# Scores of the sample attention: keys turned in place by VectorE and multiplied on sixteen array tiles

## The reference, cut to what matters

```python
kp = cache_k[page_table].reshape(DB, past, H, Dh)
vp = cache_v[page_table].reshape(DB, past, H, Dh)
suffix = (lax.cumsum(lfp, axis=1, reverse=True) - lfp).transpose(0, 2, 1)
s_past = jnp.einsum('bqhd,bkhd->bhqk', q, kp) * scale
s_past = s_past + suffix[:, :, None, :] + cn[:, :, :, None]
s_new = jnp.einsum('bqhd,bkhd->bhqk', q, k) * scale
s_new = s_new + cn[:, :, :, None] - cn[:, :, None, :]      # causal
p = softmax(concat([s_past, s_new]))
o = einsum(p[..., :past], vp) + einsum(p[..., past:], v)
```

## Time and profile before

| what | us |
|---|---|
| median of 3 runs | 1962.62 |
| lowest, highest | 1959.45, 1966.36 |
| span of the profiled execution (the page has no other time of it) | 1963.6 |
| first instruction of the stage on TensorE | 729.00 |
| last instruction of the stage | 931.96 + 0.41 = 932.37 |

### The profile page before, as it was taken

The page is one execution under the profiler, slowest core; times in us unless marked ns, Lnnn a source line. Parts: engine busy times, 40 slices in busy tenths (PEclk is TensorE's granted clock), DMA queues, the critical chain, the costliest instruction groups (busy, mean ns, idle before and its releaser), DMA issues. The chain is left out here.

```text
span 1963.6 us, 22843 instructions
## 1 busy us (share of the span) xinstructions
PE 1861.1 (95%) x8445; PEld 967.2 (49%) x8445; DVE 599.5 (31%) x1414; ACT 296.4 (15%) x514; POOL 191.5 (10%) x276
## 2 busy tenths in 40 slices
PE   8999999799999989998999997999999999996996
PEld 4454454456666555665555444544444444442442
DVE  4201124333433344553232224411111111110687
ACT  2000001122222222332110112300000000000000
POOL 2000004100000003333000000100000000000231
PEclk9999999899999998999999997999999999998898
DMA  7111110622122028999421244699999999997232
GB/s 273 16 33 57 46 49 1 245 96 70 45 91 64 30 87 290 370 382 342 177 69 66 75 177 167 241 350 425 422 420 417 429 418 418 421 424 276 90 130 96
DMA packets 108384, 407.03 MB, mean 207 GB/s; under 512 B 17433, under 2 KB 35418, under 8 KB 95986
## 3 DMA queue, kind: packets, MB, share of 16 engines
q1 hardware_dynamic: 83474, 327.59, 43.1%
q0 software_dynamic: 16496, 56.15, 7.8%
q10 hardware_dynamic: 8304, 21.84, 2.8%
HBM read 354.74 MB, written 50.79 MB: 207 GB/s over the span
## 5 line engine op out<-in xcount | busy, mean ns | idle before, releaser
L2102 PE MATMUL psum<-arena 128*64 128x512 f32 (+1 forms) x1024 | 341.1, 595 | 1.4 <-DVE arena L2196 1.4
L848 PE MATMUL psum<-arena 128*128 128x363 f32 (+1 forms) x768 | 255.7, 478 | 4.3 <-ACT arena L879 4.3
L2102 PEld LDWEIGHTS psum<-arena 128*64 128x64 f32 (+1 forms) x1024 | 129.0, 163 | 179.1 <-issue 177.3
L848 PEld LDWEIGHTS psum<-arena 128*128 128x128 f32 x768 | 140.6, 192 | 78.6 <-ACT arena L879 6.8
L2141 PE MATMUL psum<-arena 128*64 128x512 f32 (+1 forms) x512 | 170.0, 595 | 1.0 <-DVE arena L2210 1.0
L2141 PEld LDWEIGHTS psum<-arena 128*64 128x64 f32 (+1 forms) x512 | 66.1, 163 | 101.9 <-issue 101.9
L2448 PE MATMUL psum<-arena 128*128 128x512 f32 x256 | 113.8, 602 | 1.4 <-DVE arena L2485 1.4
L1563 PE MATMUL psum<-arena 128*128 128x512 f32 x256 | 113.0, 596 | 1.6 <-PEq L1398 1.6
L300 PE MATMUL psum<-arena 128*128 128x512 f32 x256 | 112.0, 594 | 0.0
L2196 DVE TENSOR_TENSOR arena<-psum,g_moe_rows 128x1024 f32<-128x1024 f32 x24 | 29.4, 1225 | 250.7 <-PE psum L2096 250.7
L1099 PE MATMUL psum<-ident,arena 128*128 128x128 f32 x512 | 82.2, 296 | 14.9 <-PEq L740 4.1
(11 more groups left out here) (289 smaller groups left out, 1946.6 us busy)
## 6 DMA issues: line engine op xcount, KB each, us to landing
arena<-in_w_exp_gate SPq DMA_DIRECT2D x32, 2048.0 KB, 13.5
arena<-in_w_exp_up SPq DMA_DIRECT2D x32, 2048.0 KB, 13.9
arena<-in_w_exp_down SPq DMA_DIRECT2D x32, 2048.0 KB, 10.5
arena<-in_cache_k SPq DMA_DIRECT2D x128, 256.0 KB, 6.7
arena<-in_cache_v POOLq DMA_DIRECT2D x128, 256.0 KB, 7.3
moe_out<-arena ACTq DMA_DIRECT2D x24, 512.0 KB, 11.9
arena<-in_w_in SPq DMA_DIRECT2D x5, 2048.0 KB, 19.9
moe_out<-arena SPq DMA_DIRECT2D x1, 10240.0 KB, 35.0
```

What stands on the lines that cost most here:

```text
L848: done = mm(c.bank[7][:, 0:b - a], WG[blk % 2][:, k, q * P:(q + 1) * P], HT[:, k, a:b], start=(k == 0), stop=(k == KD - 1))
L2102: last = mm(out[rows_, :], XT[:, u % 2, k, rows_], c.ring_tile(LOAD[kind, u, r])[:, k, :], start=(k == 0), stop=(k == KD - 1))
```

## The change

- **Keys.** VectorE transposes keys in place, in 32x32 blocks, one instruction for each chunk of 4 pages (128 partitions x 2048 numbers), straight after they land (`turn_keys`, L1232). TensorE's transposes of keys and the copies by VectorE and ScalarE are gone.
- **Scores.** After the transposition partitions 32ti to 32ti+31 hold a quarter of a head pair's dimensions for the keys 32ti to 32ti+31 of each page. A matmul has 32 rows and 16 columns and 512 keys: four quarters `dq` x four head pairs j x four key groups ti = 64 matmuls a sample (L1129), each tile (ti, j) of the array accumulating over dq in bank ti. The queries are laid out for it by ScalarE, 16 copies, once.
- **Bias.** Four matmuls of 8 rows a sample (L1116), on rows 32ti, one for each bank. Each of the four row groups gets the whole 2048 suffix sums: 4 DMAs a sample with 8 rows of 2048 numbers (64 KB each).
- **Softmax.** Scores stay in banks 0 to 3; a `tensor_reduce` over 128x2048 in PSUM takes the minimum (L1244), and ScalarE's exponential reads PSUM.
- **Own tokens.** Scores of the new tokens are made once for all samples.
- **Weights.** Their copies out of PSUM are all ScalarE's.
- **Homes.** Keys of odd samples go to a second home at `HT_AT`. SyncE issues the keys of sample b when the scores of b-2 are done. As that home is where `w_up_a` and `w_up_b` go, these are issued when all scores are done.

```diff
-    c.KC = view(c, W_AT + NCH * CH * WA, NCH, CH, WA)
+    c.KC = [view(c, W_AT + NCH * CH * WA, PAGES, WA), view(c, HT_AT, PAGES, WA)]
...
-            for b in range(DB):
+            for b in range(1, DB):
                 if b >= 2:
-                    sp.wait_ge(chunk_mm, NCH * (b - 1))
+                    sp.wait_ge(scored, b - 1)
                 for ch in range(NCH):
-                    keys = slice(ch * 512, ch * 512 + 512)
-                    sp.dma_start(SUF[bias_rows(ch), b % 2, keys], c.sufd[:, b, keys]).then_inc(bias_in[b % 2], 16)
-                if b == 0:
-                    continue
-                for ch in range(NCH):
-                    sp.wait_ge(k_tr, U * (b - 1) + NPAIR * (ch + 1))
                     c.load_keys(sp, b, ch)
+                load_bias(b)
+            sp.wait_ge(scored, DB)
             for n, w in enumerate((c.w_up_a, c.w_up_b)):
                 sp.dma_start(view(c, UP_AT + n * WBLK, KF, D), w).then_inc(c.up_in, 16)
...
+            def biases(b):
...
+                pe.wait_ge(bias_in[b % 2], 16 * NTI * (b // 2 + 1))
                 if b >= 1:
+                    pe.wait_ge(exps, 2 * b)
+                for ti in range(NTI):
+                    r = slice(32 * ti, 32 * ti + H)
+                    mm(c.bank[ti][:, :], SPREAD[r], SUF[r, b % 2, :, ti, :], start=True, stop=False,
+                       skip_group_check=True)
...
+            def scores(b):
...
+                pe.wait_ge(turned, NCH * (b + 1))
+                for dq in range(NTI):
+                    for j in range(NPAIR):
+                        cols = slice((4 * j + dq) * 32, (4 * j + dq) * 32 + 32)
+                        for ti in range(NTI):
+                            r = slice(32 * ti, 32 * ti + 32)
+                            last = mm(c.bank[ti][j * STRIP:j * STRIP + CELL, :], QB[r, b, j, dq, :],
+                                      KC[b % 2][r, :, cols], start=False, stop=(dq == NTI - 1), skip_group_check=True)
+                last.then_inc(scored, 1)
...
+            own_scores()
             for b in range(DB):
+                biases(b)
+                scores(b)
                 if b >= 2:
                     turn_out(b - 2)
                 if b >= 1:
+                    values_of(b - 1)
...
+            def turn_keys(b, ch):
+
+                dve.wait_ge(k_in[b % 2][ch], 64 * (b // 2 + 1))
+                keys = KC[b % 2][:, ch * CH:(ch + 1) * CH, :].rearrange("p g d -> p (g d)")
+                v.transpose(keys, keys).then_inc(turned, 1)
...
             def lowest(b):
                 p = b % 2
+                dve.wait_ge(scored, b + 1)
+                v.tensor_reduce(low_page[:, p:p + 1], PAGE_PS, AX.X, ALU.min).then_inc(page_low, 1)
...
             for b in range(DB):
+                for ch in range(NCH):
+                    turn_keys(b, ch)
...
                 if b >= 2:
                     out_rows(b - 2)
                     out_cells(b - 2)
+                lowest(b)
                 if b >= 1:
+                    keep_own(b - 1)
```

More of the change, by code:

```diff
@@ L980 @@
 NCH = PAGES // CH
+NTI = P // 32
+CELL = 2 * DT
 def cached_rows(c):
     c.pages = view(c, T_AT + 864, DB * PAGES).bitcast(I32)[0:1]
-    c.KC = view(c, W_AT + NCH * CH * WA, NCH, CH, WA)
+    c.KC = [view(c, W_AT + NCH * CH * WA, PAGES, WA), view(c, HT_AT, PAGES, WA)]
     c.pages_in = c.sem("pages_in")
-    c.k_in = [c.sem(f"k_in{i}") for i in range(NCH)]
+    c.k_in = [[c.sem(f"k_in{p}_{i}") for i in range(NCH)] for p in range(2)]
     def page_numbers(eng, b, ch):
@@ L1076, in _, with load_values @@
             pool.wait_ge(c.pages_in, 16)
-            for b in range(DB):
+            def load_values(b):
                 numbers = [c.page_numbers(pool, b, ch) for ch in range(NCH)]
@@ L1084, in _ @@
                                        ).then_inc(v_in[ch], 16)
+            load_values(0)
+            pool.wait_ge(cn_in, 16 * H)
+            for b in range(DB):
+                g_.tensor_tensor(NBN[:, b, :], CN, c.new_mask[:, NS - b * DT:2 * NS - b * DT],
+                                 ALU.add).then_inc(nbn_done, 1)
+            for b in range(1, DB):
+                load_values(b)
         @block.tensor
@@ L1116, in scores @@
[L1116 to L1135, removed]
@@ L1137, in own_scores @@
-            def own_scores(b):
-                pe.wait_ge(qb_done, 2 * b + 2)
-                if b >= 1:
[L1140 to L1145, removed]
+            def own_scores():
+                pe.wait_ge(qo_done, 2)
+                for b in range(DB):
+                    for j in range(NPAIR):
+                        last = mm(c.bank[7][strip(j), b * NS:(b + 1) * NS], QO[:, b, j, :], KT8[:, j, 0:NS], start=True,
+                                  stop=True)
+                last.then_inc(own_mm, 1)
@@ L1149, in turn_weights @@
                     pe.wait_ge(exps, 2 * b + 2)
[L1150 removed]
+                n = NCH * b + q
                 if n >= 2:
[L1152 to L1155, removed]
+                    pe.wait_ge(p_ev, n - 1)
+                for g in range(CH):
+                    last = tp(c.bank[4 + q % 2][:, g * P:(g + 1) * P], S[:, b % 2, CH * q + g, :], c.ident[:])
                 last.then_inc(p_tr, 1)
             def turn_own(b):
[L1159 removed]
                 if b >= 1:
                     pe.wait_ge(ot_ev, 2 * b)
[L1162 removed]
+                tp(c.bank[7][0:NS, 0:P], SN[:, b, :], c.ident[:]).then_inc(own_tr, 1)
             def weigh(b):
@@ L1256, in _ @@
             v = nc.vector
-            def qb_cells(p, half):
-                r = slice(half * DH, (half + 1) * DH)
-                cells = QB[r, p, :].rearrange("p (j n) -> p j n", n=STRIP)
-                return cells[:, :, half * DT:(half + 1) * DT]
-            def cells_of(b):
-                for half in range(2):
-                    r = slice(half * DH, (half + 1) * DH)
-                    v.tensor_scalar(qb_cells(b % 2, half), QT8[r, :, b * DT:(b + 1) * DT], 1.0, None, ALU.mult
-                                    ).then_inc(qb_done, 1)
```

235 lines of the change are left out of this document (80 added, 155 removed).

## The result

| | median us | range | runs |
|---|---|---|---|
| before | 1963.6 | 1959.5 to 1966.4 | 4 |
| after | 1984.0 | 1982.5 to 1986.8 | 4 |

The changed kernel takes 1.0105 times as long, 95% interval 1.0087 to 1.0123: 20 us more, where 1960 was forecast in a range up to 1980. In the profiled executions the span grew from 1963.6 to 1980.3 us. I measure the stage from the first issue of values to the first matmul of the merge, which waits for both up matrices: it was 738.73 to 934.83, 196.1 us, and is now 738.73 to 949.99, 211.3 us. So 15.2 of the 16.7 us lie in the one stage that was changed. The profiled executions are not the medians: the changed kernel's took 1982.5 us, its fastest run, and a span is some 2 us shorter than the time of the same execution.

A forecast was written before the change was run, and what follows sets the result against it. The DMA engines were taken to set the period, 22.3 us a sample. 740.5 + 178.4 (69.2 MB at 388 GB/s) + 8 lost = 926.9, plus 2.7 gives 929.6 against 932.4, so 1960 us; range 1951 to 1980.

The forecast's parts named there:

- the sum: Whole stage: data from 740.5, plus 178.4 us of transfers and 8 lost, so last values at 926.9 us.
- The loads: Suffix-sum DMAs: grow from 0.066 to 0.262 MB a sample, together 1.6 MB or 4 us at 388 GB/s.
- The lost time: DMA time lost to waits in the stage: 14.9 us before, taken as 8 after.
- the hole at 764: DMA at 220 GB/s from 764 to 782 us, costing 7.8 us; claimed to go as sample 2's keys issue earlier.
- some 1 us at the end comes: End of the stage: up matrices wait for the last scores, only values in flight; some 1 us of DMA time lost.
- Period: Time per sample: 8.65 MB take 22.3 us, above the chain, so set by the DMA engines; 22.19 before.
- The chain: From one sample's scores' end to those of the next: 13.0 us plus scores of 3.6 or 7.0, 16.6 to 20.0.
- The rival in which the chain becomes the bound: Worse tile overlap or dearer transpositions push the chain past 22.3 us: 1972 to 1974, or 1995 with 8 tiles; chance 0.25.
- the sign that was named for it: Sign of the chain as bound: DMA windows under 370 GB/s in the middle of the stage and scores waiting for VectorE.
- Sixteen tiles: TensorE's scores: all 16 tiles run at once, 128 records in 3.6 us a sample, 7.0 at the lower clock.
- The 10.6-fold speedup: Skill's figure for 4x4 packing, not 16: scores 5.2 us at full clock, the chain rival's first case, 1972 to 1974.
- The rate rule: The skill's about 358 GB/s of HBM for each core: bytes would take 193 us, the time near 1974.

The follow-up runs named there:

- c_skip: The changed kernel without the suffix loads of samples 2 to 7, which reuse the sums of samples 0 and 1 (computation left out): 1967.1 us.
- d_before_big: The kernel before with the changed kernel's suffix loads, four DMAs a sample of 8 rows x 2048 numbers instead of 8 x 512: 1993.5 us.
- f_layout: The changed kernel with suffix sums stored by key group, each load contiguous 8 x 512 numbers (16 KB), still behind the keys: 1968.0 us.
- l_order: f_layout with TensorE's and VectorE's order turned: values of sample b-1 weighed ahead of sample b's biases and scores: 1966.2 us.
- n_order_start: f_layout with values weighed ahead of the scores for samples 1 and 2 alone, the changed kernel's order from sample 3 on: 1971.7 us.
- h_awake: f_layout with sums issued ahead of the keys, plus 7 filler matmuls on TensorE before the scores of samples 2 to 7: 1969.7 us.
- a_quarter: The changed kernel, each row group loading only its quarter of the suffix sums in 128-byte pieces, still behind the keys: 1984.4 us.

## Why the prediction was wrong

Two terms of the sum failed, each by about half of the 24 us between 1960 and 1984. In the profiled execution TensorE's last wait for values ends at 944.35 where the sum had 926.9, 17.5 us later. The rest of the 24 lies behind it and between that execution and the medians: the sum took 1.0 us off its span for the median, where the changed kernel's median is 3.7 above its span of 1980.3.

**The loads.** "Suffix sums grow from 0.066 to 0.262 MB a sample, together 1.6 MB or 4 us at 388 GB/s". I priced their bytes at the rate of DMAs that fill 128 partitions with 2 KB each; these write 8 partitions with 8 KB each. The runs give 2.8 us (c_skip) to 3.7 us (d_before_big) for each group of four where the sum had 0.7: 16.0 to 16.9 us by f_layout and c_skip against 4, so 12 to 13 us are missing in the sum. The rows before held no DMA of this shape and size, and I gave the term no upper end, as I had given one to the transpositions.

**The lost time.** "I take 8", from 14.9 before, because the hole at 764 goes and "some 1 us at the end comes". f_layout has this change without the dear loads and the same bytes as before, 67.6 MB, 174.2 us at 388 GB/s. Its values are issued 0.7 us later than before, so data flow from some 741.2, and its last values are waited for until 932.37: 191.2 - 174.2 = 17.0 us lost, where the sum had 8. These 9 us, with what runs scatter, are the rest: f_layout's median is 12 above the 1956 that the sum gives without its 4 us of suffix bytes. Taken from the profiled executions alone, the 17.5 us are 7.8 for the loads (944.35 - 932.37, less the 4.2 that the sum had), 9.0 of lost time and 0.7 of a later start. Why the 9 us did not go is in the next points.

**Period, "22.3 us, set by the DMA engines"**: the mechanism was right, the size not. The values of samples 1 to 7 are issued from 780.52 to 923.84 us, 23.9 us apart. In f_layout they are issued from 777.79 to 911.69, 22.3 us apart, and in c_skip 21.2. With the suffix loads gone or cheap, the stretch from 784 to 900 us runs at 375 to 385 GB/s, near the 388 that the sum used.

**The hole at 764 to 782, "it goes"**: half right. Keys of sample 2 are issued early as foreseen, but the other queue was forgotten. Values of sample 1 wait for `weigh(0)`, which stands behind `scores(1)` and so behind the keys of sample 1. The changed kernel moves 270 GB/s from 764 to 782, where the sum had 388. In f_layout the hole stays at 768 to 780 with 221 GB/s, as deep as the 220 of before and 6 us shorter, and its values of sample 1 are issued at 777.79, those of before at 777.28. l_order and n_order_start, which free the values earlier, fill it, which confirms the cause; they give the gain back, so in no version was it worth the 8 us in the sum.

**"Some 1 us at the end comes"**: too small. That the up matrices wait for the last scores was in the prediction, but not that both queues run empty while the last scores run. In f_layout they rest 4 us at 29 GB/s, and before had no such rest (393 GB/s from 904 to 908).

**The chain, "16.6 to 20.0 us"**: right. In the last sample of the changed kernel, turning the output begins with the end of the scores at 900.36, the next scores start at 912.71, 12.4 us later (forecast 13.0), and take 6.80 (forecast 7.0): 19.2 us. The rival in which the chain becomes the bound is refuted by h_awake: scores shorter by up to 2.6 us, time unchanged. Half of the sign that was named for it came all the same, a middle under 370 GB/s (351), from the loads; scores waited 9.8 us for VectorE in all.

**Sixteen tiles**: right at the lower clock, a little short at the full one. 128 records take 5.6 to 7.0 us where the clock is mostly 0.50 (forecast 7.0), and 4.41 us with the clock kept at 1.00 (forecast 3.6), against 56 us in turn. The 10.6-fold speedup that I weighed as a rival ("TensorE: Matmul & The Clock Gate", Measured speedup vs the span model, of the Trainium skill) would give, as an estimate, 56 / 10.6 = 5.3 at the full clock, and the trace, 12.7-fold, is faster than that.

**The rate rule** (the Trainium skill, "DMA: Bandwidth & Descriptors", Specifications, some 358 GB/s) gave the estimate of 1974. That lies nearer to the result, but not for its reason: c_skip holds 385 GB/s over 116 us.

What stays open: which property makes the load dear, its 8 KB rows, the bytes that it puts on 8 partitions, or that four read the same source rows. The 8 partitions alone are not it, since the 16 KB loads of f_layout and a_quarter write as few and leave no such dip. f_layout changes bytes and layout at once; a load of 64 KB onto more partitions was not tried. Nor is it shown why l_order, with the start full, has only 363 GB/s in the middle.

## What to carry to other kernels

Price a DMA by a row of its own shape (bytes, partitions, piece size); where there is none, give it an upper end, and look at GB/s beside the busy share, because engines at a share of 1 may be moving half. When transfers set a stage, put last what needs the shortest chain after landing: here weights for the next stage covered the last chain, and keys last left it bare. Filling one rest of the DMA engines is a gain only if the homes that become free next can be refilled in time as well.

## What was not expected of the hardware

- Four DMAs of 64 KB onto 8 partitions each bring the DMA engines together to 184 to 260 GB/s for some 6 us, at shares of 0.99 to 1.13, while 256 KB onto 128 partitions run at 385. Packets of other transfers take longer beside them: those of values 367 ns in place of 170. The same sums as contiguous 16 KB DMAs leave no such dip in f_layout.
- A quarter of the bytes in pieces of 128 bytes removes the dip but not the lateness: in a_quarter TensorE waits 62.5 us for the sums, as long as the 61.8 for the whole, and its middle has 348 GB/s.
- In-place 32x32 transpositions on VectorE cost what the copies of the kernel before let one expect (2.3 us, from 690 ns for 512 numbers and 1.045 ns for each further one): 2285 ns for 128x2048 numbers.
